# First input passed channels-first and split straight from its load, with reordered first loads, in a hybrid attention/FFN trunk

## The reference

```
for layer in range(2):
    a = rmsnorm(h, attn_norm[layer])
    h = h + hybrid_mixer(a, w_in[layer], b_forget[layer], ...)   # 7 wide projections + 8 thin columns
    m = rmsnorm(h, ffn_norm[layer])
    h = h + (swiglu(m, dense...) if layer == 0 else moe_swiglu(m, router_w, ...))  # top 2 of 8 experts
return rmsnorm(h, final_norm)
```

## Time and profile before

| | |
|---|---|
| median of 3 runs | 2269.82 us (2269.7 to 2271.07) |
| the profiled execution, span of the core | 2270.2 us, which is 0.4 us over the median of the runs |
| its mean granted TensorE clock | 0.996 of full |
| PE busy | 2222.1 us (98%) |
| DVE, ACT, POOL busy | 69%, 55%, 17% |
| first product of PE | starts at 17.48 us |
| first thin product of PE | starts at 43.89 us |

### The profile page before, as it was taken

One profiled execution on the slowest core, in us unless ns is written; L12 is line 12 of the kernel. 1 busy time (PEld: TensorE's weight loads), 2 busy tenths in 40 slices (PEclk: granted clock), 3 DMA queues, 4 the chain that ended last, 5 costly groups with the idle time before them and its releaser, 6 DMA issues. The chain is left out here.

```text
span 2270.2 us, 29218 instructions
## 1 busy us (share of the span) xinstructions
PE 2222.1 (98%) x10255; PEld 1827.3 (80%) x10255; DVE 1565.4 (69%) x1716; ACT 1240.7 (55%) x1531; POOL 376.8 (17%) x196
## 2 busy tenths in 40 slices
PE   7999999999999999999999999999999999999997
PEld 6888888888888888888877888888877888888875
DVE  4466686666655566665554466686679999999997
ACT  5445454454444344444435445454458888887885
POOL 1111221222222222222212121121210000000001
PEclk9999999999999999999999999999999999999998
DMA  7464545555565565656554454555599999999997
GB/s 245 149 191 156 185 157 190 183 172 193 180 198 186 187 200 186 193 180 198 185 177 159 153 193 149 185 173 193 185 341 349 382 383 382 381 380 374 381 383 203
DMA packets 264462, 523.43 MB, mean 231 GB/s; under 512 B 15237, under 2 KB 19465, under 8 KB 263177
## 3 DMA queue, kind: packets, MB, share of 16 engines
q1 hardware_dynamic: 259648, 500.42, 65.0%
q0 software_dynamic: 4544, 22.03, 3.0%
q10 hardware_dynamic: 200, 0.05, 0.0%
HBM read 515.10 MB, written 15.75 MB: 234 GB/s over the span
## 5 line engine op out<-in xcount | busy, mean ns | idle before, releaser
L660 ACT ACTIVATE w_hi<-raw 128x1024 fp32r<-128x1024 f32 x744 | 778.6, 1058 | 609.0 <-PE acc L1575 558.1
L999 DVE TENSOR_TENSOR w_lo<-raw,w_hi 128x1024 fp32r<-128x1024 f32 x606 | 758.1, 1270 | 477.1 <-ACT w_hi L660 474.9
L1573 PE MATMUL acc<-w_hi,a_hi 128*128 128x512 f32 x1632 | 644.2, 395 | 3.9 <-DVE w_lo L999 2.4
L1575 PE MATMUL acc<-w_hi,a_lo 128*128 128x512 f32 x1632 | 637.0, 390 | 0.0
L1574 PE MATMUL acc<-w_lo,a_hi 128*128 128x512 f32 x1632 | 636.6, 390 | 0.0
L572 POOL TENSOR_TENSOR w_lo<-raw,w_hi 128x1024 fp32r<-128x1024 f32 x138 | 337.8, 2447 | 1304.7 <-ACT w_hi L660 1005.2
L1573 PEld LDWEIGHTS acc<-w_hi,a_hi 128*128 128x128 f32 x1632 | 307.3, 188 | 67.7 <-DVE w_lo L999 3.8
L1575 PEld LDWEIGHTS acc<-w_hi,a_lo 128*128 128x128 f32 x1632 | 307.0, 188 | 65.1
L1574 PEld LDWEIGHTS acc<-w_lo,a_hi 128*128 128x128 f32 x1632 | 307.2, 188 | 61.4
L1866 PE MATMUL acc<-w_hi,a_hi 128*128 128x512 f32 x752 | 300.5, 400 | 4.2 <-DVE w_lo L999 4.1
L1868 PE MATMUL acc<-w_hi,a_lo 128*128 128x512 f32 x752 | 293.6, 390 | 0.0
(11 more groups left out here) (237 smaller groups left out, 1497.0 us busy)
## 6 DMA issues: line engine op xcount, KB each, us to landing
raw<-in_w_in SPq DMA_DIRECT2D x112, 1024.0 KB, 5.0
raw<-in_moe_w_gate SPq DMA_DIRECT2D x64, 1024.0 KB, 10.0
more_raw<-in_moe_w_up SPq DMA_DIRECT2D x64, 1024.0 KB, 10.3
raw<-in_dense_w_gate SPq DMA_DIRECT2D x44, 1024.0 KB, 5.2
raw<-in_dense_w_up SPq DMA_DIRECT2D x44, 1024.0 KB, 5.2
raw<-in_dense_w_down SPq DMA_DIRECT2D x44, 1024.0 KB, 5.2
raw<-in_w_out SPq DMA_DIRECT2D x32, 1024.0 KB, 5.2
raw<-in_moe_w_down SPq DMA_DIRECT2D x32, 1024.0 KB, 8.2
```

What stands on the lines that cost most here:

```text
L660: nc.scalar.activation(w_hi[:, slot], raw_tile(tile)[1][:, u % TILE_UNITS], ACT.Copy)\
L999: nc.vector.tensor_tensor(w_lo[:, slot], raw_tile(u // TILE_UNITS)[1][:, u % TILE_UNITS], w_hi[:, slot].bitcast(F32), ALU.subtract).then_i ...
L1573: nc.tensor.matmul(dst, hi, w_hi[:, slot, c], start=first and c == 0, stop=False)
L1575: ins = nc.tensor.matmul(dst, lo, w_hi[:, slot, c], start=False, stop=last and c == UNIT_CHUNKS - 1)
```

## The change

The input `x` is passed a second time, as `x_t`, laid out channels-first (128 partitions x 16 chunks x 256 tokens), and all norm vectors with the forget bias come as one array `gains` in the layout that `gain` has in memory. The first eight units then build `a_hi` and `a_lo` straight from the loaded `x_t` (`first_input_hi`, `first_input_lo`), two chunks per unit, in `nat`, which nothing else uses yet. The transposes of `x` and of the gains on PE, the copy of the gains on DVE and seven of ACT's eight small DMAs go away. `x` itself is still loaded, as two blocks of 128 tokens, for the squares and the residual add. SP no longer waits for the small DMAs. Tile 0 comes as two halves. The squares move from steps 2 and 4 to steps 5 and 6, the refinement from 5 to 7. PE runs ten products of `ones` by `ones` first (`WARM`).

```diff
+XT_PIECES = (0, 2), (2, 8), (8, 16)
+WARM = 10
...
-    SQUARE_FIRST, SQUARED_FIRST = {2: 0, 4: 1}, 5
+    SQUARE_FIRST, SQUARED_FIRST = {5: 0, 6: 1}, 7
...
-            load_x(0)
+            def load_x(b):
+                sp_.dma_start(h[:, b, :], x[0, b * P:(b + 1) * P, :]).then_inc(x_in[b], 16)
+
+            def load_x_cols(n):
+                k0, k1 = XT_PIECES[n]
+                sp_.dma_start(x_cols[:, k0:k1, :], x_t[:, k0:k1, :]).then_inc(xt_in[n], 16)
...
                     if layer == 0 and j == 0:
-                        load(0, w_in[0, 0:COLS, col:col + COLS])
-                        load_x(1)
-
-                        sp_.wait_ge(small_in, 16 * N_SMALL)
-                        for t in range(1, CH // GC):
-                            load(t, w_in[0, t * COLS:(t + 1) * COLS, col:col + COLS])
-                            if t + 1 < NCOL:
-                                load_x(t + 1)
+                        load_x_cols(0)
+                        for half, landed in enumerate((first_in, loaded[0])):
+                            r = half * UNIT_CHUNKS * P
+                            sp_.dma_start(raw[:, 0, half], w_in[0, r:r + UNIT_CHUNKS * P, col:col + COLS]
+                                          .rearrange("(c p) n -> p c n", p=P)).then_inc(landed, 16)
+                        load_x_cols(1)
+                        load(1, w_in[0, COLS:2 * COLS, col:col + COLS])
+                        load_x_cols(2)
+                        load(2, w_in[0, 2 * COLS:3 * COLS, col:col + COLS])
+                        load_x(0)
+                        load(3, w_in[0, 3 * COLS:4 * COLS, col:col + COLS])
                         for l in range(DEPTH):
                             sp_.dma_start(thin[:, l], ...).then_inc(thin_in, 16)
                         sp_.dma_start(thin[:, 2], ...).then_inc(thin_in, 16)
+                        load_x(1)
                         continue
...
+            def first_input_hi(u):
+
+                if u == 0:
+                    act.wait_ge(small_in, 16)
+                for n, (k0, k1) in enumerate(XT_PIECES):
+                    if k0 == UNIT_CHUNKS * u:
+                        act.wait_ge(xt_in[n], 16)
+                for k in range(UNIT_CHUNKS * u, UNIT_CHUNKS * u + UNIT_CHUNKS):
+                    nc.scalar.activation(a_hi[:, k, :], x_cols[:, k, :], ACT.Copy,
+                                         scale=gain[:, NG_ATT + k:NG_ATT + k + 1]).then_inc(a_hi_ready, 1)
...
+            act.dma_start(gain[:, 0:NROWS + DEPTH], gains).then_inc(small_in, 16)
...
                     for u in range(LEAD):
+                        first_input_hi(u)
                         split_hi(u)
-                        if u == 0:
-                            act.wait_ge(gain_ready, 1)
-                        input_hi(0, u)
                 for u in range(ATT_UNITS):
+                    if L == 0 and u + LEAD < JOB_UNITS:
+                        first_input_hi(u + LEAD)
                     split_hi(U0 + u + LEAD)
...
+            pe.wait_ge(consts, 1)
+            for n in range(WARM):
+                nc.tensor.matmul(X[:, n % 4, 0:P], ones[:], ones[:], start=True, stop=True)
             pe.wait_ge(consts, N_CONSTS)
-            turn_input(0, 0)
...
-            pe.wait_ge(gain_ready, 1)
-            turn_input(0, 1)
-            turn_input(0, 2)
```

More of the change, by code:

```diff
@@ L66, in lin, with trunk @@
     return const if i is None else i * per + const
-def trunk(nc, x, attn_norm, w_in, b_forget, fox_q_norm, fox_k_norm, sb_out_norm, fox_out_norm, w_out,
+def trunk(nc, x, x_t, gains, w_in, w_out,
           ffn_norm, dense_w_gate, dense_w_up, dense_w_down, router_w, moe_w_gate, moe_w_up, moe_w_down,
@@ L74, in trunk @@
     CH = D // P
-    HEADS = sb_out_norm.shape[1] // P
-    W = sb_out_norm.shape[1]
+    W = (w_in.shape[2 if len(w_in.shape) == 3 else 1] * (1 if len(w_in.shape) == 3 else COLS)) // 7 // P * P
+    HEADS = W // P
     EXPERTS = router_w.shape[2]
@@ L183, in trunk @@
         silu1, hid1 = nat[:, 2, 0], nat[:, 3, 0]
+        x_cols = nat[:].rearrange("p a b n -> p (a b n)").rearrange("p (k n) -> p k n", k=CH)
         eg = sb("eg", [P, BLOCKS, COLS])
@@ L197, in trunk @@
         thin = eg[:, 0, 0:3 * P].rearrange("p (t c n) -> p t c n", t=3, c=CH)
-        rows = eg[:, 1, 0:P]
         NG_ATT, NG_FFN, NG_HEAD, NG_QK = 0, 2 * CH, 4 * CH, 4 * CH + 4 * HEADS
@@ L201, in trunk @@
         gain = sb("gain", [P, P])
+        bf = gain[0:HEADS, NROWS:NROWS + DEPTH]
         gq = sb("gq", [P, 2])
-        bf = sb("bf", [HEADS, DEPTH])
         epsc = sb("epsc", [P, 1])
@@ L272, in trunk @@
         free = [sem(f"free{s}") for s in range(2)]
-        x_in = [sem(f"x_in{c}") for c in range(NCOL)]
+        x_in = [sem(f"x_in{b}") for b in range(BLOCKS)]
+        xt_in = [sem(f"xt_in{n}") for n in range(len(XT_PIECES))]
+        first_in = sem("first_in")
         small_in = sem("small_in")
@@ L403, in h_ready @@
         def h_ready(eng, n, c):
-            if n == 0:
-                eng.wait_ge(x_in[c], 16)
-            elif n == 2:
+            if n == 2:
                 eng.wait_ge(free[1 - c % 2], att_uses[1] - 1 + c // 2)
@@ L653, in split_hi @@
                 tile = u // TILE_UNITS
-                if u % TILE_UNITS == 0:
+                if u % TILE_UNITS == 0 and u:
+                    tile_loaded(act, tile, per, i)
+                if u == 0:
+                    act.wait_ge(first_in, 16)
+                if u == 1:
                     tile_loaded(act, tile, per, i)
@@ L709, in norm_guess @@
                 rsqrt_guess(rr, ss, 2, 1.0 / D, ss_ready)
+            def first_input_hi(u):
+                if u == 0:
+                    act.wait_ge(small_in, 16)
[5 more added lines that the diff above has]
+                                         scale=gain[:, NG_ATT + k:NG_ATT + k + 1]).then_inc(a_hi_ready, 1)
             def input_hi(n, quarter):
-                act.wait_ge(xnT_ps, 4 * n + quarter + 1)
+                act.wait_ge(xnT_ps, 4 * (n - 1) + quarter + 1)
                 for k in range(4 * quarter, 4 * quarter + 4):
@@ L736, in _ @@
                     for u in range(LEAD):
+                        first_input_hi(u)
                         split_hi(u)
-                        if u == 0:
-                            act.wait_ge(gain_ready, 1)
-                        input_hi(0, u)
                 for u in range(ATT_UNITS):
+                    if L == 0 and u + LEAD < JOB_UNITS:
+                        first_input_hi(u + LEAD)
                     split_hi(U0 + u + LEAD)
-                    at_start(2 * L, u)
+                    if L:
+                        at_start(2 * L, u)
                     at_end(2 * L + 1, u - ATT_UNITS)
@@ L750, in _ @@
                         b = SQUARE_FIRST[u]
[L751 to L754, removed]
+                        act.wait_ge(x_in[b], 16)
+                        if b:
                             act.wait_ge(act_own, own.n)
@@ L1044, in one_over_rms, with first_input_lo @@
                 nc.vector.tensor_scalar(nrr, rr, -1.0, None, ALU.mult).then_inc(rr_ready, 1)
+            def first_input_lo(u):
+                if u == 0:
+                    dve.wait_ge(small_in, 16)
+                for k in range(UNIT_CHUNKS * u, UNIT_CHUNKS * u + UNIT_CHUNKS):
+                    dve.wait_ge(a_hi_ready, k + 1)
+                    nc.vector.scalar_tensor_tensor(
+                        out=a_lo[:, k, :], in0=x_cols[:, k, :], scalar=gain[:, NG_ATT + k:NG_ATT + k + 1],
+                        in1=a_hi[:, k, :].bitcast(F32), op0=ALU.mult, op1=ALU.subtract).then_inc(a_ready, 1)
             def at_start(n, u):
-                if u == 1:
+                if u == 1 and n:
                     input_lo(n, 3)
@@ L1076, in _ @@
                     dve.wait_ge(consts, N_CONSTS)
[L1078 to L1081, removed]
                     for u in range(LEAD):
+                        first_input_lo(u)
+                        if u == 0:
+                            nc.vector.tensor_scalar(gq[:], gain[:, NG_QK:NG_QK + 2], SCALE, None, ALU.mult)
                         split_lo(u)
-                        input_lo(0, u)
                 for u in range(ATT_UNITS):
+                    if L == 0 and u + LEAD < JOB_UNITS:
+                        first_input_lo(u + LEAD)
                     split_lo(U0 + u + LEAD)
@@ L1624, in _ @@
                         if j == 0:
-                            if ju == 1:
+                            if ju == 1 and L:
                                 turn_input(2 * L, 3)
@@ L1934, in _ @@
             put_rows(NCOL - 1)
-_INS = ["x", "attn_norm", "w_in", "b_forget", "fox_q_norm", "fox_k_norm", "sb_out_norm", "fox_out_norm", "w_out",
+_INS = ["x", "x_t", "gains", "w_in", "w_out",
         "ffn_norm", "dense_w_gate", "dense_w_up", "dense_w_down", "router_w", "moe_w_gate", "moe_w_up",
@@ L1948 @@
     nc = _bacc.Bacc("TRN2", target_bir_lowering=False, num_devices=1)
```

(7 more changed lines are left out.)

9 lines of the change are left out of this document (removed).

## The result

The changed kernel takes 2282.05 us (median of 4 runs, 2281.61 to 2284.96), the kernel before 2269.76 (4 runs on the same chip, 2267.45 to 2271.07): 1.0053 times as long, 95% interval 1.0042 to 1.0065. It is 12.3 us slower, where 1.6 were forecast and the range ended at 2276.0. The profiled execution of the changed kernel has a span of 2280.0 us (its time 2281.67), against 2270.2 before: the two profiles are 9.8 us apart, the medians 12.3.

The account below looks back on a forecast made before the run. PE, busy 98% of the span, was taken to bound the kernel. Thin product's moment -0.1 and clock +1.7 gave 1.6 us later, 2271.8 against the profiled 2270.2, so 2271.4 in the runs' scale; range 2265.0 to 2276.0.

Parts of the forecast that it names:

- First product at 8.6: Opening on PE: first product starts at about 8.6 us instead of 17.48, 8.9 us earlier.
- Idle products, nothing on the path: Ten WARM products at PE's start: at most 0.43 us each, 4.3 us, with nothing gained or lost.
- Unit 7 over at 31.8: Opening on PE: seven units at 2.72 us from 12.8 end at 31.8, about 9.4 us earlier than before.
- Tile 4 at 33.0: SP's load queue: tile 4, needed by unit 8, lands at T = 33.0 us, leaving PE idle from 31.8.
- the 400 GB/s: DMA ceiling in the opening, taken from measured windows; at the page's 358 GB/s T comes some 2.3 us later.
- T + 10.8: ACT and DVE chain after tile 4 lands (T): first thin product no earlier than 43.8 us, against 43.89 before.
- PE's idle time of 5.7 us ahead of it: PE finishes unit 8 at 38.1 us, then stands still 5.7 us until the first thin product.
- The clock, 1.7 of 0 to 3.4: After PE's idle spells: half clock for 3.4 us behind the thin product costs 1.7 us, bounds 0 to 3.4.
- Behind the thin product nothing is new: After the first thin product: old streams recover, units 9 to 15 taking 3.4 us each, no further cost.
- the head start: Faster rival: PE's 8.9 us earlier start lasts, gaining 9.4 us at the thin product, 2260.4 us; chance 0.15.
- Slow x loads: Slower rival: x loads in the opening delay tile 4 to 36 us or later; 2276.4 at T = 38; chance 0.15.
- Slower: Outcome case for whole-kernel time, tied to tile 4 landing from 35.9 us with the clock's 1.7; chance 0.15.

Follow-up runs that it names:

- experiment 1's kernel: Changed kernel with an unused 32-byte tile ahead of o_hi, putting o_hi and o_lo back on their old addresses: 2271.87 us, 1.0005 of the kernel before.
- the run with that edit alone: Kernel before with only an unused 32-byte tile added ahead of o_hi, moving o_hi and o_lo up by 32 bytes: 2281.71 us, 1.005.
- experiment 6: Changed kernel, o_hi/o_lo at old addresses: squares, guess, refinement at step 4, 2267.4 us; tile 4 issued earlier, squares reordered, 2260.59; the latter without idle products, 2261.63.
- experiments 3 and 5: Kernel before: 64 bytes ahead of a_hi and behind a_lo, 2312.85 us; w_hi and w_lo moved 128 bytes, 2304.92; w, a and o moved 128, 2270.6.
- experiment 4's kernel with all tiles moved: Kernel before with 128 unused bytes ahead of its first tile, so every tile moves and no distance changes: 2270.85 us, 1.0.

## Why the prediction was wrong

- **First product at 8.6:** right, 8.36. **Idle products, nothing on the path:** right; they took 4.64 us, not 4.3.
- **Unit 7 over at 31.8:** right, 32.13.
- **Tile 4 at 33.0:** right, 33.29, with the 400 GB/s behind it (414 and 396 in the windows). The Trainium skill, "DMA: Bandwidth & Descriptors", section Specifications, has about 358 GB/s there, which the trace of the changed kernel again exceeds.
- **T + 10.8:** right, 10.7 (33.29 to 43.98), link by link. The thin product was forecast at 43.8.
- **PE's idle time of 5.7 us ahead of it:** 3.72. Unit 8 ran at half clock and took its place; this moved no end.
- **The clock, 1.7 of 0 to 3.4:** mis-sized. It fell once into the wait and once, for 6.8 us, over the thin product: 2.6 us. In experiment 1's kernel, with the same opening, the second group came 5.04 behind the first instead of 3.46: 1.6. Both are inside the bounds given, and that one opening gave both shows how far this term is chance.
- **"Behind the thin product nothing is new":** this is the step that failed. I followed the instructions of the change and costed its declarations at nothing. The removal of `bf` moved `o_hi` and `o_lo` by 32 bytes, and 1824 products on them run 233.3 ns apart instead of 226.6 (12 us at the most, 10.2 by the growth of the lag, 10.6 by the run with that edit alone). With that term the sum is 1.6 + 10.6, 2282.0, and 2282.05 were measured. That it meets to 0.1 is luck in part: by the traces it is 2.7 + 10.2 - 3.0, about the 9.8 by which the two profiles differ, and two thirds of the 3.0 lie at the gather.
- **The rivals:** the head start arrived only once tile 4 and both squares were moved (experiment 6), which bears out the mechanism by which it was to be lost. Slow x loads didn't come. "Slower" had the chance of 0.15, for a cause that wasn't the one.

What stays open: why the distance matters. The runs show a rule, of pads of 32 to 512 bytes, for products of this one type and size; which access meets which wasn't shown, nor why one tile out of place costs as much as two. The 384 o products of an out projection lost 1.75 us, not the 2.6 that 384 such intervals would; and experiments 3 and 5 lost 41.6 and 33.9 us, though the a products, 7152 of them beside the 1824, went from 227.4 ns to 233.4 in the one and 232.5 in the other, which would be 53 and 46 (worked out from the starts). Most of what is missing is missing in the expert passes, the last 2256 a products: there the lag grew by 5.3 and 4.1 us, where their share would be 13.5 and 11.5. What they wait for there wasn't followed up.

## What to carry to other kernels

Read a change's declarations as well as its instructions: a tile that goes or comes moves every tile behind it, so list the addresses of PE's operands before and after. When the time moves and no wait does, take the starts of one stretch in which PE is busy throughout and compare the interval per product, operand by operand. And when a first load is made earlier, follow the queue to the next tile and the order on ACT ahead of what PE needs: here the whole 9 us lay in moving one load and in the order of squares, thin columns and refinement behind it.

## What the hardware showed that I had not expected

- Products of a 128x128 by a 128x512 tile follow each other at 226.6 ns when all stationary and moving tiles stand a multiple of 256 bytes apart in a partition, and at 232.5 to 233.3 ns otherwise, 2.5 to 3% more. Moving all operands together costs nothing (1.0 and 0.9997). One of the four tiles (`o_lo`) 32 bytes out of place costs the same 233.3 ns as two, and the products that grow longer are those ahead of its own (390 to 401 and 396 to 400 ns in mean duration, its own 391 in both).
- Ten idle products that ended 1.1 to 1.8 us ahead of the first real one had the first real ones at full pace (0.227 us) in two profiles, for three products in one, and at 0.43 us for nine products in one, as without them.
- How long the low clock lasts isn't fixed by the code: behind the same wait of 2.37 us it stood for 3.4 us in the kernel before and for 6.8 in experiment 4's kernel with all tiles moved:

```profile
1178.30:1185.10 6.80, 5.19 (x12) 4.13 (x13) 1.23 (x1) 1.24 (x2) 2.36 (x1) 0.50 0.26 69
```
